# Four down matrices of each expert stage loaded in three transfers, the last one cut at partition 119

## The chip, the cores and the metric

The kernel runs as one program on 1 core of a Trainium2 chip. The metric is the device time of one execution in microseconds (us). The kernel before takes 1586.99 us, the median of 3 runs (1585.87 to 1589.31).

## The reference

Two transformer blocks follow each other on 256 tokens of width 1024. Each has a mixer (attention and linear-attention branches in the first, two gated recurrences with a context in the second) and then a mixture of 32 experts. The change touches only how the experts' weights come in, and what each expert computes on the tokens `xb` routed to it is this (the second block has the same with `w_gate`, `w_up`, `w_down`):

```
def expert_block(args):
    toks, e = args
    xb = x[toks]
    hb = jax.nn.silu(xb @ w1[e]) * (xb @ w3[e])
    return hb @ w2[e]
...
for e in range(N_EXPERTS_2):
    a = jax.nn.silu(tok @ w_gate[e]) * (tok @ w_up[e])
    out = out + combine[:, e:e + 1] * (a @ w_down[e])
```

All is float32. Each of the three matrices of an expert is 1024 x 512 or 512 x 1024, which is 2 MB (2048 KB), so a stage reads 32 experts x 6 MB and now and then an expert twice.

## The kernel before, in words

The program runs the first mixer, the first expert stage, the second mixer and the second expert stage, in that order, on one core. The first expert stage also computes the context part of the second mixer between its experts; for it SyncE (SP) loads 1 MB pieces of `w_in_2` in lines of 2 KB (L981), with a 2 KB row of biases after four of them (L984).

An expert stage takes blocks of 32 token slots. For every expert, TensorE (PE) multiplies the gathered tokens by the two up matrices (L1555, 32 matmuls), gathers the tokens of the next expert (L1514), adds the last expert's result to the accumulators (L1522), and multiplies by the down matrix (L1582, 16 matmuls). Experts 0 to 29 (`STATIC = NE - 2`) are written out; the last experts and second blocks of a full expert run in a loop on SP's and PE's registers (L1435 and L164 issue their loads, each up matrix in two halves of 1 MB).

All weights are loaded by SP, in one queue. An expert's up matrices go to a ring of slots, two sets of slots in the first stage (`SETS` 2), three in the second (`SETS` 3); L164 issues them once PE is done with the expert whose slots they take. Down matrices rotate through buffers of their own, three at first in the first stage and then two, four in the second. `load_expert(i)` issues expert i's up matrices and then, after a wait for PE to finish a down matmul, the down matrix that comes next in that buffer, by `load_down` (L1397):

```
def load_down(i):
    e = bass.ds(i, 1)
    sp.dma_start(downs[down_at(i)].rearrange("p (o n) -> p o n", o=1),
                 W[2][0, e].rearrange("o (p k) f -> p o (k f)", k=KF)).then_inc(s_w2[down_at(i)], 16)
```

So partition p of the buffer takes 16 KB that lie together in memory, and one transfer has 128 lines of 16 KB. The semaphore rises by 16 per transfer, and PE waits for it right ahead of L1582. Nothing waits between a load and PE but that semaphore. The transfers of a queue are carried out by 16 DMA engines, each of which takes its share of the lines.

Of the kernel before, what the change touches and what calls it, by code (L numbers as in the profile page):

```python
# [12 lines left out]
P = 128  # L13
D = 1024
# [18 lines left out]
KF = FF // P  # L33
# [1250 lines left out]
def moe(c, t, w, last):  # L1284

    nc, ps, h = c.nc, c.ps, c.h
    with phase(nc, w["tag"]) as (st, sb, sem):
# [10 lines left out]
        n = sb("n", [P, TT, D])  # L1298
# [64 lines left out]
        s_w1, s_w3, s_w2 = sems[0:3 * SETS:3], sems[1:3 * SETS:3], sems[2:3 * SETS:3] + sems[3 * SETS:]  # L1363
        s_half = [sem(f"second_half_in{j}") for j in range(4)]
        downs = [c.ring[:, 2, :], c.ring[:, 5, :]] + ([third[:, 2, :]] if SETS == 3 else []) + [c.states[:, 0:KD * FF]]
        ONCE = SETS == 2
        DOWNS = len(downs) - ONCE
        LEAD = DOWNS - SETS
        ROTATE = (0, 1, 2, 0, 1, 2) if ONCE else ()
        down_at = lambda i: ROTATE[i] if i < len(ROTATE) else i % DOWNS  # L1370
# [22 lines left out]
        @block.sync  # L1393
        def _(sp):
            def load_down(i):
                e = bass.ds(i, 1)
                sp.dma_start(downs[down_at(i)].rearrange("p (o n) -> p o n", o=1),  # L1397
                             W[2][0, e].rearrange("o (p k) f -> p o (k f)", k=KF)).then_inc(s_w2[down_at(i)], 16)

            def load_expert(i):  # L1400
                u, e, done = i % SETS, bass.ds(i, 1), i - SETS + 1
                if done == 1:
                    for half in range(2):
                        sp.wait_ge((s_uph, s_up)[half], 1)
                        cs = slice(half * KD * FF // 2, (half + 1) * KD * FF // 2)
                        for which in range(2):
                            sp.dma_start(c.ring[:, which, cs].rearrange("p (o n) -> p o n", o=1),
                                         W[which][0, e].rearrange("o (p k) f -> p o (k f)", k=KD)[:, :, cs]).then_inc((s_first, sems)[half][which], 16)
                else:
                    sp.wait_ge(s_up, done)  # L1410
                    load_one(c, sp, sems, u, 0, W, e, third)
                    load_one(c, sp, sems, u, 1, W, e, third)
                later = next_down(i - SETS)
                if later is not None:
                    sp.wait_ge(s_down, done)
                    load_down(later)

            for i in range(2, 2 + LEAD + (SETS - 2)):
                load_down(i)
            if mod is not None:  # L1420
                for m in range(4):
                    at = 5 * D + m * 256
                    sp.dma_start(gate_m[32 * m:32 * m + 32, :], row_view(mod, at, at + 256, 32)).then_inc(s_gm, 16)
            sp.dma_start(frow[:], t[w["fg"]].rearrange("(o d) -> o d", o=1).to_broadcast([P, D])).then_inc(s_frow, 16)
            for i in range(SETS, STATIC):
                load_expert(i)
                if x is not None:
                    x.sp_step(sp, i)

            def load_last(u, e, done):  # L1430
                sp.wait_ge(s_up, done)
                for half in range(2):
                    cs = slice(half * KD * FF // 2, (half + 1) * KD * FF // 2)
                    for which in range(2):
                        sp.dma_start(c.ring[:, 3 * u + which, cs].rearrange("p (o n) -> p o n", o=1),  # L1435
                                     W[which][0, e].rearrange("o (p k) f -> p o (k f)", k=KD)[:, :, cs]).then_inc((sems[3 * u + which], s_half[2 * u + which])[half], 16)
                sp.wait_ge(s_down, done)
                load_one(c, sp, sems, u, 2, W, e)

            pairs = count(sp)  # L1440
            er = sp.alloc_register(w["tag"] + "expert")

            def expert_of(i):
                sp.load(er, eid_i[0:1, bass.ds(i, 1)])
                return bass.ds(sp.snap(er), 1)

            with sp.Fori(0, pairs) as q:
                for u in range(2):
                    load_last(u, expert_of(2 * q + (STATIC + u)), 2 * q + (STATIC + u - 1))
            if last:  # L1450
                o = t["out"].rearrange("b (t p) d -> p (b t) d", p=P)
                for tt in range(TT):
                    sp.wait_ge(s_end, tt + 1)
                    sp.dma_start(o[:, tt, :], n[:, tt, :]).then_inc(s_out, 16)
                sp.wait_ge(s_out, 16 * TT)
            else:
                sp.wait_ge(s_up, 2 * pairs + STATIC)
                for p in (0, 1, 3):
                    m2_load(c, sp, t, p)
                sp.wait_ge(s_down, 2 * pairs + STATIC)  # L1460
                m2_load(c, sp, t, 2)
# [28 lines left out]
        def _(pe):  # L1490
# [40 lines left out]
            def expert(i, q, u):  # L1531
                here = c.ring[:, 3 * u:3 * u + 3, :] if u < 2 else third[:]
                w13 = here[:, 0:2, :].rearrange("p w (k f) -> p w k f", k=KD)
                known = isinstance(i, int)
                down = down_at(i) if known else u
                w2 = downs[down].rearrange("p (k f) -> p k f", k=KF)

                pe.wait_ge(s_xT, i + 1)
                pe.wait_ge(s_g, i + 1)
                for k in range(KD):  # L1540
                    if known and k == 0:
                        pe.wait_ge(s_w1[u], 16 * q + 16)
                        pe.wait_ge(s_w3[u], 16 * q + 16)
                        if i == SETS:
                            pe.wait_ge(s_first[0], 16)
                            pe.wait_ge(s_first[1], 16)
                    elif not known and k % 4 == 0:
                        if k == 0:
                            pe.wait_ge(s_w1[u], 16 * q + (16 * TURNS + 16))
                            pe.wait_ge(s_w3[u], 16 * q + (16 * TURNS + 16))  # L1550
                        else:
                            pe.wait_ge(s_half[2 * u], 16 * q + 16)
                            pe.wait_ge(s_half[2 * u + 1], 16 * q + 16)
                    for j in range(4):
                        mm = pe.matmul(ps[32 * j:32 * j + 32, 4, 0:256].rearrange("p (w f) -> p w f", w=2),  # L1555
                                       xT[:, k, :], w13[:, :, k, j * P:(j + 1) * P],
                                       start=(k == 0), stop=(k == KD - 1))
                    if known and i == 0 and k == KD // 2 - 1:
                        mm.then_inc(s_uph, 1)
                mm.then_inc(s_up, 1)  # L1560
                first, second = known and i == 0, known and i == 1
                if first:
                    if x is not None:
                        x.pe_taken(pe)
                        residual()
                elif x is not None and known:
                    x.pe_early(pe, i)
                pe.wait_ge(s_Gt, i + 2)
                pe.wait_ge(s_y, i + 1)
                gather()  # L1570
                if not first:
                    pe.wait_ge(s_Gw, i + 1)
                    combine()
                    if x is not None and known and not second:
                        x.pe_main(pe, i)

                pe.wait_ge(s_gT, i + 1)
                pe.wait_ge(s_xg, i + 2)
                pe.wait_ge(s_w2[down], 16 * down_nth(i) if known else 16 * q + (16 * down_uses(u) + 16))
                for j in range(KF):  # L1580
                    for m in range(4):
                        mm = pe.matmul(ps[32 * m:32 * m + 32, 5, 0:256], gT[:, j, :],  # L1582
                                       w2[:, j, m * 256:(m + 1) * 256], start=(j == 0), stop=(j == KF - 1))
                mm.then_inc(s_down, 1)
                if first:
                    pe.wait_ge(s_slot, 1)
                    for v in range(8):
                        mm = pe.transpose(ps[:, 6 + v // 4, (v % 4) * P:(v % 4 + 1) * P], wide[:, v, :], c.ident[:])
                    mm.then_inc(s_rows, 1)
                if x is not None and second:  # L1590
                    pe.wait_ge(s_rtk, 2)
                    x.pe_gates(pe)
                    x.pe_moves(pe)
                    x.pe_main(pe, i)
# [1361 lines left out]
```

## Time and profile before

| | |
|---|---|
| median of 3 runs | 1586.99 us (1585.87 to 1589.31) |
| the profiled execution: time | 1586.88 us |
| the profiled execution: span, first to last instruction | 1585.2 us |
| mean granted TensorE clock | 0.936 |
| PE busy | 1355.3 us (85%) |
| VectorE (DVE) busy | 689.8 us (44%) |
| ScalarE (ACT) busy | 246.0 us (16%) |
| DMA | 529.59 MB, 334 GB/s over the span |

Busy times are per engine and overlap. The DMA share of a stretch is the part of the time of all 16 DMA engines in which they carried packets: 0.56 is nine of sixteen busy. Packets are put to the stretch in which they start, so a short stretch can show a share over 1. "Us to landing" is from the issue on SP to the last part's arrival. In the order listings, `128x4096` is lines x float32 elements of a line.

### The profile page before, as it was taken

To read this page: it belongs to the slowest core of one execution; us is meant where nothing else is said; L and a number is where in the kernel's file an instruction comes from. 1 tells how busy PE (TensorE), PEld (TensorE's weight loads), DVE (VectorE), ACT (ScalarE), POOL (GpSimd) and SP (SyncE) were. 2 spreads that over 40 slices of the span, in tenths; PEclk is the share of its full clock that TensorE was granted. 3 is DMA by queue.
4 is the path that set the end of the run, shared out by engine and by line. 5 is a ranking of instruction groups with operands and counts; after the bars stand their busy time and mean duration, and the time that the engine had idled before them with its cause. 6 is when DMAs were issued, how large, how long until landed. Compare 5 with 4: busy or idle time off the path is not lost. (4 is left out here: it accounts for less than half of the span.)

```text
span 1585.2 us, 27653 instructions
## 1 busy us (share of the span) xinstructions
PE 1355.3 (85%) x11904; PEld 877.8 (55%) x11904; DVE 689.8 (44%) x1844; ACT 246.0 (16%) x501; POOL 79.9 (5%) x125
## 2 busy tenths in 40 slices
PE   9999988989878798799999999999886656666665
PEld 8655555544455566488767748886443333333333
DVE  4634655323223342427687536652553233233324
ACT  2322230100001111132222113230200000000000
POOL 2401000000000000030000100100000000000000
PEclk9999999999989999999999999999998788788878
DMA  9965799999999999977523444474999999999996
GB/s 335 273 224 196 309 413 428 391 424 429 425 429 425 424 428 426 385 246 280 200 98 115 147 173 159 164 287 202 391 428 427 429 428 428 429 428 428 428 424 260
DMA packets 94328, 529.59 MB, mean 334 GB/s; under 512 B 8312, under 2 KB 10640, under 8 KB 67968
## 3 DMA queue, kind: packets, MB, share of 16 engines
q1 hardware_dynamic: 89080, 522.35, 81.5%
q0 software_dynamic: 2624, 5.32, 1.5%
q8 instruction: 94, 1.54, 0.4%
q10 hardware_dynamic: 2504, 0.16, 0.1%
q14 instruction: 26, 0.21, 0.0%
HBM read 526.74 MB, written 1.07 MB: 333 GB/s over the span
## 5 line engine op out<-in xcount | busy, mean ns | idle before, releaser
L1555 PE MATMUL ps<-weight_ring,e_xT 128*32 128x256 f32 x3456 | 251.6, 454 | 135.7 <-DMA weight_ring<-in_w_up_dram 92.3
L1555 PEld LDWEIGHTS ps<-weight_ring,e_xT 128*32 128x32 f32 x3456 | 138.2, 130 | 244.9 <-issue 199.8
L1810 DVE TENSOR_TENSOR e_g<-e_act_g,ps 128x128 f32<-128x128 f32 x64 | 24.8, 388 | 269.3 <-ACT e_act_g L1627 268.2
L1808 DVE TENSOR_TENSOR e_act_g<-e_act_g,ps 128x128 f32<-128x128 f32 x32 | 9.2, 286 | 240.8 <-ACT e_act_g L1627 240.8
L1627 ACT ACTIVATE e_act_g<-ps 128x128 f32<-128x128 f32 x64 | 17.8, 278 | 581.4 <-PE ps L1555 581.4
L1582 PE MATMUL ps<-weight_ring,e_gT 128*32 128x256 f32 x1536 | 93.8, 385 | 3.3 <-DMA weight_ring<-in_expert_w_dram 2.0
L1555 PE MATMUL ps<-expert_set,e_xT 128*32 128x256 f32 x640 | 51.6, 493 | 46.5 <-DMA expert_set<-in_w_up_dram 46.5
L2329 PE MATMUL ps<-expert_set,weight_ring 128*128 128x256 f32 x384 | 84.2, 379 | 0.0
L2329 PEld LDWEIGHTS ps<-expert_set,weight_ring 128*128 128x128 f32 x384 | 73.0, 190 | 9.9
L1522 PE MATMUL ps<-e_y,e_GwT 32*128 32x256 f32 x1024 | 74.8, 407 | 2.1 <-DVE e_y L1842 1.6
L1514 PE MATMUL ps<-e_n,e_Gt 128*32 128x256 f32 x1056 | 70.8, 384 | 3.4 <-DVE e_Gt L1760 2.0
L1582 PEld LDWEIGHTS ps<-weight_ring,e_gT 128*32 128x32 f32 x1536 | 46.4, 110 | 47.8 <-issue 20.4
L1555 PEld LDWEIGHTS ps<-expert_set,e_xT 128*32 128x32 f32 x640 | 29.3, 140 | 68.5 <-issue 63.0
L1522 PEld LDWEIGHTS ps<-e_y,e_GwT 32*128 32x128 f32 x1024 | 47.1, 187 | 30.5 <-issue 27.0
L1118 PE MATMUL ps<-ctx_early,e_nT 128*128 128x512 f32 x128 | 59.8, 616 | 4.0 <-DVE e_ctx_kw L1237 4.0
L1126 PE MATMUL ps<-e_nT,ctx_early 128*128 128x256 f32 x256 | 57.4, 382 | 0.0
L2195 PE MATMUL ps<-weight_ring,expert_set 128*128 128x512 f32 x128 | 56.2, 592 | 0.0
L2291 PE MATMUL ps<-weight_ring,expert_set 128*128 128x512 f32 x128 | 55.7, 593 | 0.0
L2182 PE MATMUL ps<-expert_set,weight_ring 128*128 128x256 f32 x256 | 55.4, 379 | 0.0
L1126 PEld LDWEIGHTS ps<-e_nT,ctx_early 128*128 128x128 f32 x256 | 48.0, 190 | 8.9 <-issue 2.7
L2182 PEld LDWEIGHTS ps<-expert_set,weight_ring 128*128 128x128 f32 x256 | 48.6, 190 | 6.6
L1514 PEld LDWEIGHTS ps<-e_n,e_Gt 128*32 128x32 f32 x1056 | 34.4, 110 | 26.0 <-issue 5.5
(591 smaller groups left out, 1923.7 us busy)
## 6 DMA issues: line engine op xcount, KB each, us to landing
weight_ring<-in_expert_w_dram SPq DMA_DIRECT2D x88, 2048.0 KB, 20.8
weight_ring<-in_w_in_dram SPq DMA_DIRECT2D x26, 2048.0 KB, 10.0
weight_ring<-in_w_gate_dram SPq DMA_DIRECT2D x19, 2048.0 KB, 33.2
weight_ring<-in_w_up_dram SPq DMA_DIRECT2D x19, 2048.0 KB, 37.7
weight_ring<-in_w_down_dram SPq DMA_DIRECT2D x18, 2048.0 KB, 39.3
weight_ring<-in_w_ada_dram SPq DMA_DIRECT2D x12, 2048.0 KB, 12.6
expert_set<-in_w_gate_dram SPq DMA_DIRECT2D x10, 2048.0 KB, 33.7
expert_set<-in_w_up_dram SPq DMA_DIRECT2D x10, 2048.0 KB, 38.1
```

The source lines that it names most:

```text
L1118: mm = pe.matmul(ps[:, b, :], nT[:, k8, (b - 6) * P:(b - 5) * P], w[:, k, :], start=(k8 == 0), stop=(k8 == KD - 1), skip_group_check=True)
L1126: mm = pe.matmul(ps[:, b, j * T:(j + 1) * T], w[:, k, at:at + P], nT[:, k8, :], start=(k8 == 0 and j == 0), stop=(k8 == KD - 1), skip_grou ...
L1514: mm = pe.matmul(ps[32 * j:32 * j + 32, 5, 0:256], Gt[:, tt, :], n[:, tt, j * 256:(j + 1) * 256], start=(tt == 0), stop=(tt == TT - 1))
L1522: mm = pe.matmul(ps[:, m, tt * 256:(tt + 1) * 256], GwT[r, tt * P:(tt + 1) * P], y[r, :], start=False, stop=False, skip_group_check=True)
L1555: mm = pe.matmul(ps[32 * j:32 * j + 32, 4, 0:256].rearrange("p (w f) -> p w f", w=2), xT[:, k, :], w13[:, :, k, j * P:(j + 1) * P], start= ...
L1582: mm = pe.matmul(ps[32 * m:32 * m + 32, 5, 0:256], gT[:, j, :], w2[:, j, m * 256:(m + 1) * 256], start=(j == 0), stop=(j == KF - 1))
L1627: act.activation(act_g[:], ps[:, 4, 0:P], gated).then_inc(s_silu, 1)
L1810: dve.tensor_tensor(g[:], spread(act_g[:]), spread(ps[:, 4, P:2 * P]), ALU.mult).then_inc(s_g, 1)
L2182: mm = pe.matmul(ps[:, 4 + j % 4, 0:T], w[:, k, (j % 4) * P:(j % 4 + 1) * P], nT[:, k, :], start=(k == 0), stop=(k == KD - 1))
L2195: mm = pe.matmul(ps[:, 6 + j % 2, :], nT[:, k, tile * P:(tile + 1) * P], w[:, k, :], start=(k == 0), stop=(k == KD - 1))
L2291: mm = pe.matmul(ps[:, j % 4, :], nTp[:, k, tile * P:(tile + 1) * P], w[:, k, :], start=(k == 0), stop=(k == KD - 1))
L2329: mm = pe.matmul(ps[:, 2 + f % 2, 0:T], w[:, k, j * P:(j + 1) * P], rhs[:, k, :], start=(k == 0), stop=(k == KD - 1))
```

## The change

In each of the two expert stages, the down matrices of experts 6, 12, 18 and 24 come in three transfers in place of one. The first has all 128 lines but only their first seven eighths (3584 float32, 14 KB). The second has the last eighth (512 float32, 2 KB) of partitions 0 to 118, the third that of partitions 119 to 127. The second and third count on a semaphore of their own, `s_rest`, and PE waits for both (32 more each time) ahead of the down matmul of such an expert.

```
+        UNEVEN = (6, 12, 18, 24)
+        s_rest = sem("rest_of_down_in")
...
             def load_down(i):
                 e = bass.ds(i, 1)
-                sp.dma_start(downs[down_at(i)].rearrange("p (o n) -> p o n", o=1),
-                             W[2][0, e].rearrange("o (p k) f -> p o (k f)", k=KF)).then_inc(s_w2[down_at(i)], 16)
+                dst, src = downs[down_at(i)].rearrange("p (o n) -> p o n", o=1), W[2][0, e].rearrange("o (p k) f -> p o (k f)", k=KF)
+                if i not in UNEVEN:
+                    sp.dma_start(dst, src).then_inc(s_w2[down_at(i)], 16)
+                    return
+                main = 7 * KF * D // 8
+                sp.dma_start(dst[:, :, 0:main], src[:, :, 0:main]).then_inc(s_w2[down_at(i)], 16)
+                for a, b in ((0, 119), (119, P)):
+                    sp.dma_start(dst[a:b, :, main:], src[a:b, :, main:]).then_inc(s_rest, 16)
...
                 pe.wait_ge(s_w2[down], 16 * down_nth(i) if known else 16 * q + (16 * down_uses(u) + 16))
+                if known and i in UNEVEN:
+                    pe.wait_ge(s_rest, 32 * UNEVEN.index(i) + 32)
```

No matmul and no operation of another engine is added, taken away or moved. On SP's queue, in the first stage, the down matrix of expert 6 stands between the up matrices of two experts. Before:

```order
L164 DMA weight_ring<-in_expert_w_dram 128x4096 x2
L1397 DMA weight_ring<-in_expert_w_dram 128x4096
L164 DMA weight_ring<-in_expert_w_dram 128x4096 x2
L1397 DMA weight_ring<-in_expert_w_dram 128x4096
```

With the change:

```order
L164 DMA weight_ring<-in_expert_w_dram 128x4096 x2
L1404 DMA weight_ring<-in_expert_w_dram 128x3584
L1406 DMA weight_ring<-in_expert_w_dram 119x512
L1406 DMA weight_ring<-in_expert_w_dram 9x512
L164 DMA weight_ring<-in_expert_w_dram 128x4096 x2
L1401 DMA weight_ring<-in_expert_w_dram 128x4096
```

The whole load of expert 6 has become three issues at the same place, and everything behind it on the queue is two issues later.

## Rows read from the trace of the kernel before

**Rows 1.** The page: span, the 40 slices of TensorE, granted clock and DMA
```profile
span 1585.2 us, 27653 instructions
...
PE   9999988989878798799999999999886656666665
...
PEclk9999999999989999999999999999998788788878
DMA  9965799999999999977523444474999999999996
GB/s 335 273 224 196 309 413 428 391 424 429 425 429 425 424 428 426 385 246 280 200 98 115 147 173 159 164 287 202 391 428 427 429 428 428 429 428 428 428 424 260
```

**Rows 2.** Busy time by stretch: both expert stages, then a stretch of 2 KB lines
```profile
core 0: us, PE busy (x) PEld busy (x) DVE busy (x) ACT busy (x) POOL busy (x), PEclk, DMA share, GB/s
...
300.00:470.00 170.00, 149.35 (x1549) 79.12 (x1551) 43.88 (x153) 13.68 (x35) 0.00 (x0) 0.93 1.01 426
470.00:655.00 185.00, 158.32 (x1828) 107.96 (x1819) 73.13 (x220) 28.36 (x72) 0.00 (x0) 0.95 1.01 426
...
1300.00:1450.00 150.00, 95.69 (x1280) 52.77 (x1280) 45.62 (x150) 2.78 (x10) 0.00 (x0) 0.82 1.01 429
...
30.00:38.00 8.00, 8.00 (x39) 7.04 (x38) 0.00 (x0) 0.77 (x2) 0.00 (x0) 1.00 1.05 386
```

**Rows 3.** Who waited for whom in the second stage, 1150 to 1575 us
```profile
PE ps L1555 <- DMA weight_ring<-in_w_up_dram: 92.3, 18, 7.2
PE ps L1555 <- DMA expert_set<-in_w_up_dram: 46.5, 9, 6.0
```

**Rows 4.** DMA queues, first stage (205 to 668 us): packets, MB, share
```profile
q1 hardware_dynamic: 21434, 193.43, 99.4%
q8 instruction: 35, 0.57, 0.5%
q14 instruction: 8, 0.07, 0.0%
...
ctx_early<-in_w_in_dram SPq DMA_DIRECT2D x16, 1024.0 KB, 20.4
```

**Rows 5.** The same in the second stage (1150 to 1572 us)
```profile
q8 instruction: 32, 0.52, 0.5%
...
weight_ring<-in_w_down_dram SPq DMA_DIRECT2D x15, 2048.0 KB, 39.4
```

**Rows 6.** By stretch, how the DMA engines run out at the second stage's end
```profile
1564.00:1565.00 1.00, 0.07 (x3) 0.00 (x0) 0.00 (x0) 0.00 (x0) 0.00 (x0) 0.50 0.67 279
1565.00:1566.50 1.50, 0.40 (x5) 0.23 (x8) 0.00 (x0) 0.00 (x0) 0.00 (x0) 0.50 0.67 284
1566.50:1569.50 3.00, 3.00 (x40) 1.74 (x36) 0.00 (x0) 0.10 (x1) 0.00 (x0) 0.62 0.55 235
1569.50:1571.00 1.50, 1.50 (x32) 0.85 (x20) 1.22 (x4) 0.18 (x1) 0.00 (x0) 1.00 0.10 33
```

**Rows 7.** The same at the first stage's end
```profile
659.00:660.00 1.00, 1.00 (x16) 0.57 (x12) 0.00 (x0) 0.00 (x0) 0.00 (x0) 0.50 0.99 418
...
660.00:661.50 1.50, 1.01 (x12) 0.17 (x4) 0.00 (x0) 0.00 (x0) 0.00 (x0) 0.72 0.76 322
661.50:664.50 3.00, 2.14 (x40) 1.60 (x44) 0.00 (x0) 0.15 (x1) 0.00 (x0) 1.00 0.57 243
```

**Rows 8.** In order of time: the waits of TensorE at both ends
```profile
662.36 1.93 PE L1555 MATMUL ps<-weight_ring,e_xT 128*32 128x256 f32 x32 [1.35 <-DMA weight_ring<-in_expert_w_dram]
...
667.24 1.93 PE L1582 MATMUL ps<-weight_ring,e_gT 128*32 128x256 f32 x32 [1.01 <-DMA weight_ring<-in_expert_w_dram]
...
1566.10 3.24 PE L1555 MATMUL ps<-weight_ring,e_xT 128*32 128x256 f32 x32 [2.03 <-DMA weight_ring<-in_w_up_dram]
...
1571.20 1.93 PE L1582 MATMUL ps<-weight_ring,e_gT 128*32 128x256 f32 x32
```

**Rows 9.** By stretch, a gap of the queue in the first stage
```profile
276.00:281.00 5.00, 5.00 (x40) 2.12 (x42) 0.00 (x0) 0.00 (x0) 0.00 (x0) 1.00 0.78 331
281.00:283.00 2.00, 2.00 (x44) 1.17 (x36) 0.00 (x0) 0.38 (x1) 0.00 (x0) 1.00 0.60 123
```

**Rows 10.** SP's queue in order of time, 225 to 300 us
```profile
231.73 0.33 SPq L1397 DMA_DIRECT2D weight_ring<-in_expert_w_dram  x1
...
250.67 11.81 SPq L164 DMA_DIRECT2D weight_ring<-in_expert_w_dram  x4
281.32 0.33 SPq L1397 DMA_DIRECT2D weight_ring<-in_expert_w_dram  x1
281.69 0.43 SPq L981 DMA_DIRECT2D ctx_early<-in_w_in_dram  x1
```

## Prediction

> **What bounds the kernel now.** I read the page's slices first. The DMA row shows two long stretches of nines, slices 6 to 16 and 29 to 39, nearly all at over 420 GB/s: these are the two expert stages, and TensorE's clock is full or nearly so in the first and at 7 or 8 tenths in the second [rows 1]. By stretch, the DMA share is 1.01 in both while TensorE is busy for 149 of 170 us and for 96 of 150 [rows 2]. In the second stage TensorE's wait for an up matrix comes to 92.3 + 46.5 = 138.8 us [rows 3]. So the bytes set the pace, and the last one to land sets the end of a stage: at the first stage's end TensorE waits 1.35 us for up weights and 1.01 us for the last down matrix; at the second's it waits 2.03 us for the last up half, and starts the last down matmuls 1.9 us after those 3.24 us are over, with only the gather and the combine between [rows 8].
>
> A share of 1.01 hides that the 16 DMA engines are not equally far. When SP has nothing more in its queue, the second stage's share doesn't drop from 1 to 0. It is 0.67 for 2.5 us, then 0.55 for 3 us, then 0.10 [rows 6]. 0.55 x 16 is nine engines. So seven engines run out of work early, the last of them at about 1566, and nine carry on until about 1570.4. The first stage ends the same way: 0.99, then 0.76, then 0.57 for 3 us [rows 7], with the last bytes used at 667.24 [rows 8]. I take the lead of the slowest of the seven over the slowest of the nine as 4.5 us at both ends; the stretches allow 3.8 to 5.3.
>
> What makes it: beside the loads, the queue of instruction fetches (q8) moves 35 packets in the first stage and 32 in the second, 0.5% of 16 engines' time [rows 4, 5]. That is 0.005 x 463 x 16 = 37 us of one engine, 1.06 us a packet, and 34 us in the second stage. Spread over nine engines it is 4 us each, spread over sixteen it would set nobody back against another. The size fits a lead of 4.5 us that grows over a stage.
>
> **The change, part by part.**
>
> Bytes and matmuls stay the same; what moves is who carries them. A whole down matrix is 8 lines of 16 KB for each engine. At 429 GB/s [rows 2] that is 8 x 16384 x 16 / 429000 = 4.89 us. The first transfer, 8 lines of 14 KB, is 4.28 us. Then 119 lines of 2 KB. 119 is 7 x 17, so I take it that seven engines carry 17 each; the last nine lines give one each to nine engines, which I take to be the first seven and two more.
>
> What a 2 KB line costs: the stretch where only such lines run has 386 GB/s [rows 2], 16 x 2048 / 386000 = 0.085 us. In the first stage 16 pieces of 1 MB in 2 KB lines, 8.7% of the 193 MB [rows 4], bring the rate only from 429 to 426 [rows 2], which solves to 397 GB/s or 0.083 us. I take 0.083 and keep 0.080 and 0.085.
>
> A round then costs the seven engines 4.28 + 18 x 0.083 = 5.77 us, which is 0.88 more than before, and the others 0.61 less (the two with one line more, 0.53).
>
> Second stage, four rounds: the seven end 4 x 0.88 = 3.5 us later, so 1.0 us ahead of where the slowest ended before; the nine end 2.4 us earlier. The seven now set the end. Gain: 1.0 us.
>
> First stage, only three rounds count. Expert 6's down matrix is issued at 231.73, and between the issues of 250.67 to 262.48 and that of 281.32 SP issues nothing [rows 10]; the share falls to 0.78 and 0.60 [rows 9]. All engines run dry and start together, so what round 6 has shifted is lost there. Three rounds: the seven end 2.6 us later, 1.9 ahead of the old end, the nine 1.8 us earlier, or 1.6 where it is one of the two. Gain: 1.7 us.
>
> Two more issues on SP in each of eight places take 0.33 to 0.43 us each [rows 10], 0.8 us by which what follows on the queue is later. A load of these stages lands 39.4 us after its issue in the second stage and a 1 MB piece 20.4 us after in the first [rows 4, 5], so the queue hides it: nothing. If that cover were gone, as at 281 us, it would be 0.8 us once; no split load stands right there. The wait on `s_rest` costs TensorE nothing of its own. In the first rounds the seven lead by less than they will later, so a tail could land later than the whole matrix did, by at most 0.88 us; in a stage that is set by the queue this is made up by its end. Behind each stage the chain is as it was: whatever the last landing gains, all that follows gains.
>
> Sum: 1.0 + 1.7 = 2.7 us off the profiled execution's own 1586.88 us: 1584.2. The median of the runs is 0.1 us above that execution, so I compare with 1587.0. Ends: a lead of 3.8 us and 0.085 a line give 0.1 + 1.0 = 1.1 us; a lead of 5.3 and 0.080 give 2.0 and the nine's 1.7, 3.7 us. This case alone is 1583.2 to 1585.8.
>
> The rows don't show which engines carry an odd number of lines. The Trainium skill ("DMA: Bandwidth & Descriptors", "Why a DMA increments its semaphore by 16 and not by 1") says that the engine count is the largest number up to 16 that divides the outer dimension, which makes 7 of 119 and 9 of 9, and that it is the lowest-numbered ones. No row here shows it.
>
> **The rivals.**
>
> *No relief on the receiving side.* If what limits is not the engine that carries a line but the part of the on-chip memory that takes it, the nine gain nothing: the bytes into their partitions are the same. Then 0 us, 1586.9. For it: 16 KB lines hold 429 GB/s through the whole stage, as if at a fixed limit [rows 2]. Against: fetch packets hold up the engine that carries them although they bring nothing to those partitions. The Trainium skill ("SBUF — State Buffer", "Door 1: The DMA port swizzle") has this rule: a port serves eight partitions and takes about 27 GB/s. By it the case is this one. Chance 0.17.
>
> *The 119 lines go to all sixteen engines*, seven or eight each. Then the change doesn't shift anything: 1586.9. Chance 0.05.
>
> *The tails are the new last part.* Place: the 17 lines of each of the seven, written across partitions into which the other engines are writing at full rate. If two writers share there, a line takes 0.166 us, a round 4.28 + 2.99 - 4.89 = 2.38 us more. Second stage 9.5 - 4.5 = 5.0 us later, first 7.1 - 4.5 = 2.6 us: 1594.5. It decides from 0.096 us a line, where four rounds use up 4.5 us. Against it: the 2 KB lines of the first stage run among 16 KB lines at 0.083. But those are spread evenly, as 119 over seven are not. Chance 0.11.
>
> *The seven that get the lines aren't the seven that are ahead.* The rows show seven ahead and that 119 is 7 x 17, not that these are the same. If those behind are loaded, the ends come 3.5 and 2.6 us later: 1593.0. Chance 0.09; that both numbers are seven speaks against it.
>
> **How the numbers follow.** The forecast has a chance of 0.58. A measurement of this kernel tells about 0.2% from no change, 3.2 us; the three runs before lie 3.4 us apart. The forecast's 2.7 us is under that; with its own range and about 1 us of scatter in a median, 0.22 of the 0.58 comes out faster by over 0.2%, and 0.02 of the cases without effect do: faster 0.24. Slower is the last two rivals less the weak part of them, 0.18. Within 0.2%: 0.58. The range is 1582.5 to 1589.5: it holds the forecast and both cases without effect with their scatter, and leaves out most of the two slow ones.
>
> **What would show it.** At both ends the stretches show the plateau near 0.56 gone or under 2 us, and the share falls from 1 to 0 within about 3 us. TensorE's last down matmuls start 1.7 us earlier in the first stage (667.24) and 2.7 in the second (1571.20). If the plateau of nine stays, the receiving side limits or the seven are the wrong ones, and the last landing tells these apart (unmoved, or some 3 us later). If a plateau of three to seven engines stands at the end, the tails are too long. The forecast is wrong if the second stage's last down matmuls start later than 1570.5.

## The result: slower by 19 us

| | before | with the change |
|---|---|---|
| median of 5 runs | 1587.45 us (1585.87 to 1589.31) | 1606.55 us (1604.54 to 1608.26) |
| ratio, 95% interval | | 1.0121 [1.011, 1.0132] |
| profiled execution, its span | 1586.88, 1585.2 us | 1608.26, 1606.5 us |
| mean granted clock | 0.936 | 0.928 |

The forecast was 1584.2 us, in a range of 1582.5 to 1589.5. The change costs 19.1 us, and 21.3 us between the two profiled spans. Places within the kernel are told by the two profiled executions.

The page with the change, to hold against [rows 1]:

```profile
span 1606.5 us, 27677 instructions
...
PEclk9999999999899999899999999999997878788878
DMA  9955799999999999867523444585999999999995
GB/s 334 275 212 209 299 418 415 414 413 427 424 411 428 407 425 425 345 230 282 202 102 110 145 170 157 182 297 210 390 413 427 428 409 427 411 429 408 428 408 241
```

The share of busy DMA engines is as full as before. The bytes per second aren't: slices at 427 to 429 alternate with slices at 407 to 414. Engines that are "busy" as much and move fewer bytes are being held up. One stretch of 4 us after the other, around the landing of expert 6's down matrix in the second stage (columns as in [rows 2]: us, busy PE, PEld, DVE, ACT, POOL, granted clock, DMA share, GB/s):

```profile
1190.00:1194.00 4.00, 1.75 (x32) 0.78 (x24) 3.79 (x12) 0.00 (x0) 0.00 (x0) 1.00 1.02 436
1194.00:1198.00 4.00, 1.52 (x16) 0.91 (x20) 1.21 (x7) 0.00 (x0) 0.00 (x0) 0.60 0.98 417
1198.00:1202.00 4.00, 4.00 (x44) 2.10 (x40) 0.00 (x0) 0.00 (x0) 0.00 (x0) 0.55 1.08 324
1202.00:1206.00 4.00, 4.00 (x72) 2.34 (x68) 2.84 (x10) 0.28 (x1) 0.00 (x0) 1.00 0.98 396
...
1283.00:1303.00 20.00, 8.72 (x128) 4.79 (x128) 5.22 (x19) 0.28 (x1) 0.00 (x0) 0.85 1.01 388
1303.00:1343.00 40.00, 28.45 (x380) 16.15 (x384) 11.82 (x40) 0.83 (x3) 0.00 (x0) 0.77 1.01 428
```

Where the tails run, the whole core's transfers fall to 324 GB/s at a share of 1.08. A stretch of 4 us is rough, since a packet counts where it starts; but over the 20 us around the next tail (1283 to 1303) the rate is 388 at a share of 1.01 as well. In a stretch without a tail (1303 to 1343) it is 428, as in [rows 2].

The ends of both stages, again by stretch, to hold against [rows 7] and [rows 6]:

```profile
667.00:668.00 1.00, 1.00 (x12) 0.27 (x4) 0.00 (x0) 0.00 (x0) 0.00 (x0) 0.50 0.79 336
668.00:669.50 1.50, 0.28 (x4) 0.00 (x0) 0.00 (x0) 0.00 (x0) 0.00 (x0) 0.50 0.45 191
669.50:672.00 2.50, 1.94 (x20) 1.13 (x24) 0.00 (x0) 0.00 (x0) 0.00 (x0) 0.50 0.18 79
672.00:674.00 2.00, 2.00 (x24) 1.02 (x20) 0.00 (x0) 0.24 (x1) 0.00 (x0) 0.50 0.12 49
...
1584.00:1586.00 2.00, 0.12 (x4) 0.00 (x0) 0.00 (x0) 0.00 (x0) 0.00 (x0) 1.00 0.84 356
1586.00:1588.00 2.00, 0.85 (x12) 0.64 (x16) 0.00 (x0) 0.00 (x0) 0.00 (x0) 0.83 0.32 135
1588.00:1590.00 2.00, 2.00 (x25) 1.22 (x20) 0.00 (x0) 0.00 (x0) 0.00 (x0) 0.50 0.18 74
1590.00:1592.00 2.00, 2.00 (x32) 1.24 (x28) 0.93 (x3) 0.28 (x1) 0.00 (x0) 0.82 0.06 25
```

The plateau of nine at 0.55 is gone, as forecast. In its place there is one at 0.18, and 0.18 x 16 = 2.9: about three engines are still at work when the others have finished. The prediction had named this sign ("a plateau of three to seven engines"), for the rival of tails that are too long. The experiments show that only a part of it is that.

TensorE in order of time at both ends, to hold against [rows 8]:

```profile
670.06 3.64 PE L1563 MATMUL ps<-weight_ring,e_xT 128*32 128x256 f32 x32 [1.78 <-DMA weight_ring<-in_expert_w_dram]
...
676.69 1.93 PE L1592 MATMUL ps<-weight_ring,e_gT 128*32 128x256 f32 x32
...
1587.14 3.53 PE L1563 MATMUL ps<-weight_ring,e_xT 128*32 128x256 f32 x32 [3.03 <-DMA weight_ring<-in_w_up_dram]
...
1592.63 1.93 PE L1592 MATMUL ps<-weight_ring,e_gT 128*32 128x256 f32 x32
```

**The 21.3 us by place.** (1) The first stage's last up half starts at 670.06 in place of 662.36: 7.7 us for three rounds. (2) These 32 matmuls then take 3.64 us in place of 1.93, since the granted clock is 0.50 (1.2 GHz) in the rows from 667 to 674, where it was 1.00 (2.4 GHz) in [rows 7], and the last down matmuls start 9.4 us late (676.69 against 667.24): 1.7 us more. (3) The matmuls of L2388 (L2398 now), the last long group ahead of the second stage, start 10.7 us late: 1.3 us more. That is the clock again. Behind the stage, 16 matmuls take longer, and the granted clock around them (from 688 to 692 us) is 0.70 where it was 1.00. First before, then with the change:

```profile
679.04 1.97 PE L2164 MATMUL ps<-ident,expert_set 128*128 128x128 f32 x16 [2.13 <-DVE expert_set L2579]
```

```profile
688.51 2.67 PE L2174 MATMUL ps<-ident,expert_set 128*128 128x128 f32 x16 [2.14 <-DVE expert_set L2589]
...
688.00:692.00 4.00, 3.49 (x19) 3.30 (x20) 2.30 (x6) 2.82 (x6) 3.92 (x5) 0.70 1.05 386
```

Of the thirteen kernels of this case, the six in which these 16 matmuls take 2.7 to 3.6 us are 1.3 us later there; in the seven in which they take 1.96 or 1.97 us, nothing is lost between the stages. (4) The second stage's last down matmuls are late by 1592.63 - 1571.20 = 21.4 us, so the stage itself adds 10.7 us, for four rounds.

Each place is read from one execution of each kernel. In kernels that are unchanged up to the second stage, the first stage's last down matmuls start 2.7 us earlier to 0.3 us later than in the kernel before, so a place is good to some 3 us.

A round thus costs 2.6 us in the first stage and 2.7 in the second, where the forecast had the end gain.

### The profile page after: what moved, and what is told of

Its sections match the earlier page's. It is cut to its first block and busy times, and to the rows that moved or that the text cites. A ratio compares the mean times of both kernels' runs of the same rounds, so it can differ in the third digit from the quotient of the medians.

```text
span 1606.5 us, 27677 instructions
## 1 busy us (share of the span) xinstructions
PE 1361.5 (85%) x11904; PEld 881.4 (55%) x11904; DVE 689.0 (43%) x1844; ACT 246.0 (15%) x501; POOL 80.1 (5%) x125
```

## The experiments

Two theories, both of them rivals in the prediction. **A:** the uneven tails are slow, because engines write across partitions that other engines are filling. **B:** the seven engines that carry the 119 lines aren't the seven that are ahead. The expectations have a third, **C:** lines of 2 KB cut out of longer ones, or the transfers added, are slow in themselves. A difference in what follows is that of the medians against the kernel before on the same chip; the experiments ran on three chips, and the kernel before has 1586.05, 1586.15 and 1586.9 us on them.

**The tail in one transfer of 128 lines.** Eight lines of 2 KB for each engine: a main part, a tail and the wait for it, without the unevenness.

```
-                for a, b in ((0, 119), (119, P)):
+                for a, b in ((0, P),):
...
-                    pe.wait_ge(s_rest, 32 * UNEVEN.index(i) + 32)
+                    pe.wait_ge(s_rest, 16 * UNEVEN.index(i) + 16)
```

> The same four experts, the same first transfer of 14 KB lines, but the last eighth in one transfer of all 128 lines, so that every DMA engine carries eight of them, into the partitions it also fills otherwise. Theory A (the loss comes from DMA engines that write into partitions which others are filling at full rate): nothing is shared here, so 0 to +1 us (8 rounds of 8 lines at 0.083 in place of 0.076 us, +0.5). Theory B (the seven that got 17 lines are those that were behind already): the shares are even, so 0 to +1 us. Theory C (2 KB pieces cut out of 16 KB rows, or the two more transfers, are slow in themselves): most of the change's +19 us stays, +10 us or more, with the rate dipping at each split.

1587.31 against 1586.05 us, ratio 1.0005 [0.9995, 1.0015]. The 2 KB lines, one issue more and the wait cost nothing that can be told from no change. What costs 19 us comes with the cut at partition 119: in how the lines are dealt out, or in a third transfer.

**The tail cut in the middle.** With 64 lines in each transfer I take it that all sixteen engines carry four, twice. Then nothing is shifted between engines; only which partitions an engine writes at a time changes.

```
-                for a, b in ((0, 119), (119, P)):
+                for a, b in ((0, 64), (64, P)):
```

> Three transfers again, but the last eighth is cut at partition 64: 64 lines and 64 lines, four of each for every one of 16 engines. No engine has more lines than another; but each half is written by all sixteen into half of the partitions. Theory A: two writers wherever a line goes, so a line costs 0.15 to 0.17 in place of 0.083 us, 8 lines 0.6 us more in each of 8 rounds: +3 to +6 us, and 16 KB packets beside them last longer than 0.61 us. Theory B: the shares are even: 0 to +1 us. Theory C: as the change itself, +10 us or more.

1600.02 against 1586.05 us, 1.0083 [1.0062, 1.0104]: 14.0 us, where A had been given 3 to 6 and C 10 or more. Its stretches at the same tail, with the 50 us around it, and under them those of the tail in one transfer:

```profile
1190.00:1194.00 4.00, 0.75 (x8) 0.46 (x12) 1.09 (x6) 0.00 (x0) 0.00 (x0) 0.56 0.98 416
1194.00:1198.00 4.00, 4.00 (x48) 2.20 (x44) 0.00 (x0) 0.00 (x0) 0.00 (x0) 0.59 1.07 335
1198.00:1202.00 4.00, 4.00 (x75) 2.33 (x68) 2.61 (x10) 0.28 (x1) 0.00 (x0) 1.00 0.97 379
1170.00:1220.00 50.00, 36.91 (x560) 20.54 (x553) 23.52 (x79) 1.11 (x4) 0.00 (x0) 0.86 1.01 416
```

```profile
1186.00:1190.00 4.00, 3.60 (x36) 2.06 (x40) 0.00 (x0) 0.00 (x0) 0.00 (x0) 0.50 0.98 415
1190.00:1194.00 4.00, 4.00 (x75) 2.30 (x71) 1.68 (x5) 0.28 (x1) 0.00 (x0) 0.99 1.06 452
1170.00:1220.00 50.00, 32.57 (x477) 18.14 (x477) 19.91 (x67) 0.83 (x3) 0.00 (x0) 0.84 1.01 427
```

Same bytes and same line size, but over the 50 us around a tail 416 GB/s against 427, which is 1.3 us of transfer. The single stretches of 4 us spread too much for a size. In the changed kernel the same 50 us have 416 GB/s as well. So the loss needs no shift between engines and has nothing to do with 119. This run alone can't tell A from C's "one transfer more"; the next pair and the tails of half the size do. The Trainium skill ("DMA: Bandwidth & Descriptors", "Rules for kernel authors") says of two transfers to disjoint halves of the partitions: don't bother, they serialize. The run is harder than the rule: the split costs 14.0 us over seven tails that count, 2.0 us each. By place, in its own trace, it is 5.6 us at the first stage's last up half, 1.9 us more behind it by the clock (0.6 and 1.3, as in (2) and (3) above), and 6.7 us in the second stage. Without the clock that is 12.3 us, 1.8 a round:

```profile
667.96 3.43 PE L1563 MATMUL ps<-weight_ring,e_xT 128*32 128x256 f32 x32 [3.01 <-DMA weight_ring<-in_expert_w_dram]
...
673.45 1.93 PE L1592 MATMUL ps<-weight_ring,e_gT 128*32 128x256 f32 x32
...
1101.79 27.73 PE L2398 MATMUL ps<-weight_ring,m_FT 128*128 128x512 f32 x64 [0.97 <-DVE m_FT L2894]
...
1585.33 1.93 PE L1592 MATMUL ps<-weight_ring,e_gT 128*32 128x256 f32 x32
```

**Seven engines loaded, with nothing split.** To the kernel before are added four transfers of 7 lines of 4 KB, at eleven experts of the second stage, into a tile that is free there. I take that to be one line for each of the seven engines a time, 44 lines or 44 x 4096 x 16 / 429000 = 6.7 us for each over the stage. In the first version the lines go to partitions 0, 4, ... 24 and the three next to each, every other time 32 higher; in the second to the same, 64 higher. The source is the same in both.

```
+        EXTRA = (6, 8, 10, 12, 14, 16, 18, 20, 22, 24, 26) if SETS == 3 else ()
+        OFFS = (0, 1, 2, 3)
+        s_extra = [sem(f"extra_in{j}") for j in range(2)]
+        spare = wide.rearrange("p a b -> p (a b)")
...
+                if i in EXTRA:
+                    turn, half = divmod(EXTRA.index(i), 2)
+                    if turn:
+                        sp.wait_ge(s_extra[half], 16 * len(OFFS) * turn)
+                    for a in OFFS:
+                        a += 32 * half
+                        at, of = slice(0 + a, 25 + a, 4), slice(0 + a, 25 + a, 4)
+                        sp.dma_start(spare[at].rearrange("p (o n) -> p o n", o=1),
+                                     W[2][0, e].rearrange("o (p k) f -> p o (k f)", k=KF)[of, :, 0:1024]).then_inc(s_extra[half], 16)
...
+            for half in range(2):
+                if EXTRA:
+                    sp.wait_ge(s_extra[half], 16 * len(OFFS) * len(EXTRA[half::2]))
```

and in the second version

```
-                        at, of = slice(0 + a, 25 + a, 4), slice(0 + a, 25 + a, 4)
+                        at, of = slice(64 + a, 89 + a, 4), slice(0 + a, 25 + a, 4)
```

> The kernel before, with transfers added in the second stage alone: eleven rounds (at the down matrices of experts 6, 8 .. 26) of four transfers of seven 4 KB lines each, from rows of the down matrix into an idle buffer, at partitions 0, 4 .. 24 (then 1, 5 .. 25, and so on; every other round 32 higher). The seven engines that carry such a transfer are taken to be those that fill these partitions anyway. 11 x 4 x 0.16 = 7.0 us more work for each of the seven. If they are the seven that are ahead by 4.5 us (theory A): +2 to +3 us. If they are among those behind (theory B): +7 us.

> The same as the one before it, same source rows, same sizes, same engines, but written to partitions 64, 68 .. 88 and those beside and 32 above them, which other engines fill. Theory A: each of these groups of partitions has to take 11 x 4 x 4 KB = 180 KB more beside its own full stream, 6.8 us at 26.6 KB/us: those behind end 7 us or more later, +7 to +14 us, 4 us or more above the run before it, and 16 KB packets last up to 1.2 us beside the added lines. If it doesn't matter where a line goes: the same as the run before it, within 1 us.

The first: 1592.61 against 1586.05 us, 1.0042 [1.0029, 1.0054], 6.6 us. That is the whole 6.7 us that each of the seven has more to do. Had all seven been 4.5 us ahead, some 2.2 would have come out; had all sixteen engines shared the lines, 11 x 28 x 4096 / 428000 = 2.9. B is real too. The second: 1607.45, 1.0134 [1.0107, 1.016], 21.4 us. The same bytes by the same engines at the same moments cost 14.8 us more when they are written 64 partitions higher. The number of transfers is the same in both, so this is A and not C. It is also more than the expectation's +7 to +14 us: if a group of partitions merely took its bytes at a fixed rate, the lines added would hold it up by 6.7 us. Why it is over twice that, no run shows. The second stage by stretch, first of the one, then of the other, and the kernel before last:

```profile
1160.00:1530.00 370.00, 240.19 (x3268) 131.17 (x3260) 120.67 (x397) 7.22 (x26) 0.00 (x0) 0.82 1.01 428
```

```profile
1160.00:1530.00 370.00, 230.69 (x3148) 126.34 (x3140) 116.08 (x382) 6.95 (x25) 0.00 (x0) 0.81 1.01 412
```

```profile
1160.00:1530.00 370.00, 241.44 (x3324) 134.22 (x3320) 120.61 (x397) 7.23 (x26) 0.00 (x0) 0.83 1.01 428
```

With the first version the rate stays at 428 through the stage: its 6.6 us are all at the end, where a few engines are late. With the second the rate itself is 412, so engines that got nothing more to do are slowed as well: 370 us at 412 in place of 428 are 13.8 us of transfer, nearly all of the 14.8.

The choice of the two sets follows the Trainium skill ("SBUF — State Buffer", "Door 1: The DMA port swizzle"): a port serves a group of four partitions and the group 32 above it, and 64 higher lies the other port of the same cluster. The two runs agree with it. No run maps the ports one by one.

**How many of the seven are behind.** The same extra load for the first four, the first two, the first one and, later, the first three engines, at the same partitions as in the version without contention.

```
-                        at, of = slice(0 + a, 25 + a, 4), slice(0 + a, 25 + a, 4)
+                        at, of = slice(0 + a, 13 + a, 4), slice(0 + a, 13 + a, 4)
```

(5 + a for two, 1 + a for one, 9 + a for three.)

> As e3_own (added 4 KB lines into partitions that their engine fills anyway, eleven rounds of four in the second stage), but transfers of four lines, partitions 0, 4, 8, 12, so that four engines get 7.0 us more. e3_own came out 6.6 us slower, with three of sixteen engines still at work for 6 us at the end: three of its seven engines are behind already and set the end. If one of those three is among these four: +7 us again, and the plateau at the end is as many engines as are behind among the four. If none is: the four end 7.0 - 4.5 = 2.5 us late, +2 to +3 us.

> The same with two lines, partitions 0 and 4: two engines get 7.0 us more. +7 us if either is behind already, +2 to +3 us if neither is.

> The same with one line, partition 0: one engine gets 7.0 us more. +7 us if it is behind already, +2 to +3 us if it is one of those ahead.

> As e6_two with three lines, partitions 0, 4, 8: three engines get 7.0 us more, into their own partitions. Two came to +1.2 us and four to +6.9, so one of the third and the fourth engine is behind. If it is the third: +7 us. If the fourth: +1 to +3 us, as with two.

| engines loaded | us against the kernel before | ratio, interval |
|---|---|---|
| one | +1.4 | 1.0008 [0.9998, 1.0018] |
| two | +1.2 | 1.0011 [0.9998, 1.0024] |
| three | -0.6 | 0.9995 [0.9985, 1.0005] |
| four | +6.9 | 1.0042 [1.0028, 1.0057] |
| seven | +6.6 | 1.0042 [1.0029, 1.0054] |

Up to three engines take 6.7 us more with no difference that the intervals tell from none, less than the +2 to +3 (or +1 to +3) expected for engines that are ahead; the fourth brings the whole of it at once. All five have the same number of transfers, so that number costs nothing here. Seven ran on one chip, one, two and four on a second, three on a third: that the fourth engine is the first late one assumes that the chips are alike in this, as the end times of the kernel before are. The runs with four, then with seven engines loaded, by stretch at the second stage's end:

```profile
1572.00:1574.00 2.00, 0.73 (x13) 0.51 (x17) 0.00 (x0) 0.00 (x0) 0.00 (x0) 0.95 0.10 41
1574.00:1576.00 2.00, 2.00 (x24) 1.34 (x20) 0.00 (x0) 0.00 (x0) 0.00 (x0) 0.50 0.10 33
1576.00:1578.00 2.00, 2.00 (x25) 1.12 (x20) 0.89 (x3) 0.28 (x1) 0.00 (x0) 0.69 0.04 16
```

```profile
1570.00:1572.00 2.00, 0.54 (x12) 0.24 (x12) 0.00 (x0) 0.00 (x0) 0.00 (x0) 0.89 0.26 111
1572.00:1574.00 2.00, 2.00 (x44) 1.47 (x40) 0.00 (x0) 0.28 (x1) 0.00 (x0) 1.00 0.22 90
```

0.10 x 16 = 1.6 engines are late with four loaded, and 0.22 to 0.26 x 16 = 3.5 to 4.2 with seven. With the plateau of 2.9 in the changed kernel I read it as about three of the seven, the fourth and two of the fifth to seventh; which two was not tried, and the shares would also allow all three. And three loaded engines leave the last down matmuls where they were, at 1571.27 against 1571.20:

```profile
1571.27 1.93 PE L1598 MATMUL ps<-weight_ring,e_gT 128*32 128x256 f32 x32 [0.99 <-DMA weight_ring<-in_w_down_dram]
```

So the lead of the first three is some 6 us or more, and not 4.5. [Rows 6] allow it: the share is 0.67 from 1564 on, eleven engines, so five had run dry 6.4 us or more before 1570.4.

**Contention without B.** The two engines that are surely ahead carry the extra lines, written 64 partitions higher.

```
-                        at, of = slice(0 + a, 5 + a, 4), slice(0 + a, 5 + a, 4)
+                        at, of = slice(64 + a, 69 + a, 4), slice(0 + a, 5 + a, 4)
```

> As e6_two (two engines, both ahead, carry 7.0 us more of 4 KB lines in the second stage; into partitions of their own this came to +1.2 us), but written to partitions 64 and 68 and the ones beside and 32 above, which two other engines fill. Same source rows, same engines, same sizes. If writing where another engine writes costs nothing of its own: +1 to +3 us, as e6_two. If the two groups of partitions take what comes at a fixed rate of about one engine's full stream (26.8 KB/us): their 180 KB more each hold up the engines that fill them by 6.7 us, which gives +7 us if one of these two is behind already and +2 to +3 us if both are ahead; the two carriers, slowed as well, may add to that: up to +10.

1592.69 against 1586.9 us, 1.004 [1.0026, 1.0053], 5.8 us, where the same two lines a time in the other partitions cost 1.2. It lies between what was expected with both carriers ahead (+2 to +3) and the +7 of a late one. The rate over 1160 to 1530 us is 421 GB/s here and 428 there:

```profile
1160.00:1530.00 370.00, 235.30 (x3244) 129.38 (x3236) 119.75 (x395) 6.96 (x25) 0.00 (x0) 0.83 1.01 421
```

```profile
1160.00:1530.00 370.00, 240.78 (x3329) 132.54 (x3325) 120.89 (x398) 7.23 (x26) 0.00 (x0) 0.82 1.01 428
```

So A costs time even when only engines with time to spare write across: whoever fills those partitions is slowed, and it may be one that sets the end.

**Only one round a stage.**

```
-        UNEVEN = (6, 12, 18, 24)
+        UNEVEN = (12,)
```

> The change, but in each stage only for expert 12: one round in place of four. If the loss is made at each split and stays (contention while the tails run, and three of the seven engines being among those behind), a round costs (1606.55 - 1587.45) / 7 to 8 = 2.4 to 2.7 us, twice: +4.5 to +5.5 us. If it came from something else that the change brings once, such as the wait on a second semaphore or the shift of SP's queue, it stays near +19 us or goes to 0.

1590.89 against 1586.15 us, 1.003 [1.0019, 1.0041]: 4.7 us for two rounds, 2.4 each, as expected (+4.5 to +5.5). The cost is by the round from the first one on; there is no lead that the first round could use up.

**Tails of half the size.**

```
-                main = 7 * KF * D // 8
+                main = 15 * KF * D // 16
```

> The change, but with 15 sixteenths in the first transfer and the last sixteenth cut at partition 119: lines of 1 KB in place of 2 KB, as many of them. If the cost goes by the bytes that seven engines carry into partitions of others: half of the change's +19 us, +8 to +11 us. If it goes by transfers and lines: it stays at +15 to +19 us.

1594.23 against 1586.9 us, 1.0046 [1.003, 1.0062]: 7.3 us, a little under the +8 to +11 expected. Half the bytes cost 0.4 of the time, so the price goes with the bytes in the tails, and not with the number of transfers or lines, which is the same. With the 44 transfers that cost nothing above, that leaves nothing of C. In its worst 4 us the rate is 373 GB/s and not 324:

```profile
1194.00:1198.00 4.00, 4.00 (x56) 2.29 (x52) 0.00 (x0) 0.09 (x1) 0.00 (x0) 0.67 1.02 373
```

**The sum.** Seven rounds count, since the first stage's first is lost in the gap. B: 7 x 0.88 = 6.2 us, by the prediction's own price for a round. A: the 12.3 us of the cut in the middle without the clock. The clock: 1.7 + 1.3 = 3.0 us. Together 21.5 us, against 21.3 between the two spans. Cut at 119 instead of 64 the contention needn't be the same, and a place is good to some 3 us, so the sum shows that the three are enough, not that each has its exact size.

## Why the prediction was wrong

- **That the seven engines with the 119 lines are the seven that are ahead failed.** This is the first step that failed; that nine are late and that seven carry the tail are not contradicted by any run. It had been put as a rival at 0.09 with "that both numbers are seven speaks against it". The number was a coincidence: the first three are ahead, the fourth is late, and by the plateaus so are about two of the next three. The late ones carry 0.88 us more a round, so the stage's end moves by the full 0.88 a round instead of gaining 1.0 and 1.7 us. That rival priced such a load at its full size (3.5 + 2.6 = 6.1 us), and the seven loaded engines measured just that: 6.6 us for a load of 6.7.
- **The 2 KB line at 0.083 us is the second.** It came from lines that are dealt out evenly, in [rows 2] and [rows 4], and it holds there: the even tail costs nothing. Of uneven tails no row showed anything; the prediction saw this ("those are spread evenly, as 119 over seven are not") and still gave the rival 0.11. Contention measured 1.8 us a round in the cut at 64 (2.0 with what the clock added). In the changed kernel itself, 10.7 less 3.5 us over four rounds is 1.8 a round, and 7.7 less 2.6 over three is 1.7.
- **The rivals were priced apart, and both came true.** 1593.0 and 1594.5 each stopped at the one mechanism. The range ended at 1589.5, since it treated them as exclusive and cut them off. The tails' rival also let four rounds use up a lead of 4.5 us first (5.0 and 2.6 us left); as the late engines had no lead, nothing was used up.
- **"No relief on the receiving side"** (0.17) had the right part of the chip and the wrong sign. It took the receiving side as a limit that stays even. When one engine writes into partitions that another fills, it takes from that one, and more than its own bytes would: 14.8 us for a load of 6.7.
- **What held.** The bytes set the pace and the last landing the end. Expert 6's round in the first stage leaves no trace behind the gap: SP issues the next down matrix at 281.63 where it was 281.32 [rows 10], and the kernel that splits expert 12 alone has it at 281.44. The issues and the wait on `s_rest` cost nothing: the even tail has one more issue and the wait, and the kernels with one to three loaded engines have 44 more issues.

```profile
250.06 11.60 SPq L164 DMA_DIRECT2D weight_ring<-in_expert_w_dram  x4
281.63 0.33 SPq L1401 DMA_DIRECT2D weight_ring<-in_expert_w_dram  x1
```

- **What was not in any case:** 3.0 us by the clock: 1.7 at the first stage's end, where TensorE waits longer and its last up matmuls run at 1.2 in place of 2.4 GHz, and 1.3 behind it. No run shows what brings the lower clock at the second place; it comes in six of the thirteen kernels.

Is there a version that gains? None of the eleven runs points to one. Shifting work away from the late engines takes an uneven transfer, and with its lines where others write, even the two engines ahead cost 5.8 us. As long as a matrix keeps its place, a line taken from a late engine goes into that engine's partitions by another one, so I saw no version without contention to try.

## What to carry to other kernels

A plateau in the drain tells how many engines are ahead, not which. Before building on which engine is which, load a few of them with a known number of lines and see from which one on the end moves; here it took four small runs. And where all DMA engines are busy, keep each transfer on all 128 partitions: cutting its lines shorter cost nothing here, cutting it by partitions cost 2 us a time. The price of such a cut is not its issues but that engines then write into partitions that others are filling, and that slows the engines that you did not touch.

## What the hardware did that I had not expected

- Engines that write into partitions which others are filling slow the whole stream: for a tail of 256 KB cut at 64 the 50 us around it run at 416 GB/s, and uncut at 427. 28 lines of 4 KB at a time, over eleven experts, take a 370 us stretch from 428 to 412 GB/s or leave it at 428, by their destination alone.
- The lag between engines is uneven. Over the second stage the first three engines gain at least some 6 us on the slowest, and the fourth nothing. The instruction fetches of [rows 4, 5] were my explanation of it; no run tested it, and it stays open.
- The DMA share doesn't fall when engines are held up by each other: it read 1.08 in the stretch with the lowest rate. Only GB/s beside it shows the loss.
